# Feed-forward projections: one 512-column product for the weights' high part, and token factors moved to x's update

## The reference

```python
# first block (D_MODEL = 1024, D_FF = 4096)
h = rmsnorm(x, norm_mlp_g[i])
x = x + jnp.square(jax.nn.relu(h @ w_ff1[i])) @ w_ff2[i]
...
# second block, twice in each of its two layers (D_FF_2 = 2816, FFN_RES_WEIGHT = 0.5)
def swiglu(x, w_gate, w_up, w_down):
    return (jax.nn.silu(x @ w_gate) * (x @ w_up)) @ w_down

for layer in range(2):
    x = x + 0.5 * swiglu(rms_norm(x, norm_ffn1[layer]), ffn1_w_gate, ffn1_w_up, ffn1_w_down)
    xn = rms_norm(x, norm_mix[layer])
    x = x + mix(xn) @ w_out[layer]
    x = x + 0.5 * swiglu(rms_norm(x, norm_ffn2[layer]), ffn2_w_gate, ffn2_w_up, ffn2_w_down)
```

## Time and profile before

| what | value |
|---|---|
| median of 3 runs | 1515.05 us (1514.81 to 1521.53) |
| profiled execution, its own time | 1521.02 us |
| its span in the trace | 1519.2 us |
| TensorE busy | 1475.0 us (97%) |
| VectorE busy | 982.9 us (65%) |
| ScalarE busy | 721.0 us (47%) |
| mean granted TensorE clock | 0.991 |
| moved by DMA | 249.28 MB, mean 164 GB/s |

### The profile page before, as it was taken

The page is one execution under the profiler, slowest core; times in us unless marked ns, Lnnn a source line. Parts: engine busy times, 40 slices in busy tenths (PEclk is TensorE's granted clock), DMA queues, the critical chain, the costliest instruction groups (busy, mean ns, idle before and its releaser), DMA issues.

```text
span 1519.2 us, 25531 instructions
## 1 busy us (share of the span) xinstructions
PE 1475.0 (97%) x11068; PEld 1341.1 (88%) x11068; DVE 982.9 (65%) x1260; ACT 721.0 (47%) x864; POOL 0.2 (0%) x4
## 2 busy tenths in 40 slices
PE   7999999999998899998998999999999999899999
PEld 6999898998887899888778999899998777699987
DVE  5875577876457766557766665476654785576653
ACT  6743474543356543346555343363443564444432
POOL 0000000000000000000000000000000000000000
PEclk9999999999999999999999999999999998999999
DMA  7441135655544555544334555555555344155552
GB/s 301 158 163 58 57 112 194 211 173 195 193 164 141 193 193 172 190 166 167 134 116 159 176 193 179 189 184 174 191 182 190 127 164 142 30 192 185 176 194 83
DMA packets 35823, 249.28 MB, mean 164 GB/s; under 512 B 4096, under 2 KB 4224, under 8 KB 6144
## 3 DMA queue, kind: packets, MB, share of 16 engines
q1 hardware_dynamic: 35712, 247.65, 47.4%
HBM read 246.58 MB, written 1.05 MB: 163 GB/s over the span
## 4 chain that ended last, share of the span: by engine, by line
PE 93%; DVE 3%; ACT 2%; issue 1%; DMA 0%; SPq 0%; ACTq 0%; DVEq 0%
PE ps L1731 28%; PE ps L1733 28%; PE ps L1732 28%; PE ps L1861 2%; DVE lo L2413 1%; PE ps L1782 1%; ACT hi L2083 1%; PE ps L2028 1%; PE ps L2055 1%; PE ps L1890 1%; PE ps L2044 1%; PE ps L2036 1%; DMA X<-xin 0%; PE ps L1847 0%; PE ps L1985 0%
## 5 line engine op out<-in xcount | busy, mean ns | idle before, releaser
L2083 ACT CAST hi<-raw 128x2048 fp32r<-128x2048 f32 x230 | 437.8, 1905 | 556.7 <-PE ps L1733 553.5
L2413 DVE TENSOR_TENSOR lo<-raw,hi 128x2048 fp32r<-128x2048 f32 x230 | 526.4, 2290 | 268.0 <-ACT hi L2083 267.8
L1731 PE MATMUL ps<-HH,hi 128*128 128x256 f32 x2032 | 585.6, 288 | 19.6 <-DVE lo L2413 18.9
L1732 PE MATMUL ps<-HL,hi 128*128 128x256 f32 x2032 | 578.6, 285 | 0.0
L1733 PE MATMUL ps<-HH,lo 128*128 128x256 f32 x2032 | 578.5, 285 | 0.0
L1731 PEld LDWEIGHTS ps<-HH,hi 128*128 128x128 f32 x2032 | 393.5, 194 | 24.7 <-DVE lo L2413 20.7
L1732 PEld LDWEIGHTS ps<-HL,hi 128*128 128x128 f32 x2032 | 393.5, 194 | 0.2
L1733 PEld LDWEIGHTS ps<-HH,lo 128*128 128x128 f32 x2032 | 393.2, 193 | 0.0
L1731 PE MATMUL ps<-hi,a 128*128 128x512 f32 x584 | 231.1, 396 | 0.0
L1733 PE MATMUL ps<-hi,a 128*128 128x512 f32 x584 | 231.0, 396 | 0.0
L1732 PE MATMUL ps<-lo,a 128*128 128x512 f32 x584 | 229.9, 394 | 0.0
(11 more groups left out here) (310 smaller groups left out, 1200.1 us busy)
## 6 DMA issues: line engine op xcount, KB each, us to landing
raw<-ws SPq DMA_DIRECT2D x230, 1024.0 KB, 4.8
X<-xin SPq DMA_DIRECT2D x8, 256.0 KB, 6.4
const<-const SPq DMA_DIRECT2D x1, 1348.0 KB, 10.8
out<-X SPq DMA_DIRECT2D x4, 256.0 KB, 2.3
small<-small SPq DMA_DIRECT2D x1, 992.5 KB, 12.5
a<-row SPq DMA_DIRECT2D x1, 512.0 KB, 6.1
a<-pin SPq DMA_DIRECT2D x1, 256.0 KB, 5.3
const<-const SPq DMA_DIRECT2D x1, 64.0 KB, 2.6
```

Source lines behind the costliest of these rows:

```text
L1731: e.matmul(o, ah, bh, start=start, stop=False)
L1732: e.matmul(o, ah, bl, start=False, stop=False)
L2083: e.copy(hi[j % NSPL][:, :], raw[j % NRAW][:, :]).then_inc(hi_ready, 1)
L2413: e.tensor_tensor(lo[j % NSPL][:, :], raw[j % NRAW][:, :], hi[j % NSPL][:, :].bitcast(F), ALU.subtract).then_inc(lo_ready, 1)
```

## The change

- `HH` and `HL` become the two halves of one tensor `h2`. For gate, up and `w_ff1` a step (k, u) has two matmuls: the high part of the weights by both parts of h, 512 columns into a whole bank (first half high by high, second half high by low), and the low part of the weights by `HH`, 256 columns onto the first half. So each piece uses two banks.
- At the eviction the halves are added: ScalarE copies the second half of each bank to SBUF (new kind `half`), VectorE adds the first half to it (`add_halves`).
- The token factor is no longer applied to `up` and `relu`. `x_add` of the down projection multiplies with 0.5 * rstd or rstd squared instead, taken from columns that `n_root` and `f_end` now compute. `gate` still needs it ahead of the sigmoid and has a pass of its own for that. `relu` now squares in the same VectorE operation as the maximum, and ScalarE copies in place of squaring.
- `rows_into_x` clears `weaving[0]` before the next norm's parts follow.
- All other column pieces (23 of them) keep `cols_piece`.

```diff
-        HH = fixed("HH", [128, 8, S], R)
-        HL = fixed("HL", [128, 8, S], R)
+        h2 = fixed("h", [128, 2, 8, S], R)
+        HH, HL = h2[:, 0, :, :], h2[:, 1, :, :]
...
+        by_half = [st[:, 12:13], st[:, 13:14]]
+        by_square = [st[:, 14:15], st[:, 15:16]]
...
+        half_to = {"relu": rl, "gate": sgm, "up": ups}
...
-            emit("cols", pe=FINE * 0.36, i=i, a=j + 128 * u, o=0 if alone else u, k0=k, nk=nk, src=src, slot=slot,
-                 opens=k == 0 and (alone or u == 0), closes=k + FINE == nk and (alone or u == 1),
+            emit("wide" if wide else "cols", pe=FINE * 0.36, i=i, a=j + 128 * u, o=u, k0=k, nk=nk, src=src, slot=slot,
+                 opens=k == 0 and (wide or u == 0), closes=k + FINE == nk and (wide or u == 1),
...
+        def second_half(kind, slot, c, u, over):
+            return emit("half", act=0.4, slot=slot, to=kind, j=(c // 256) % 2, u=u, over=over, v=half_a.add())["v"]
+        def wide_piece(name, layer, c, needs, begin, evac):
+            piece_check(name, layer, 0, c)
+            i = next_piece[0]
+            yield from split(i)
+            sls = []
+            for u in range(2):
+                yield from room(1)
+                sls.append(take())
+                for k in range(0, 8, FINE):
+                    cols_step(i, 0, u, k, 8, "h", sls[u], needs, True)
+                    if k + FINE < 8:
+                        yield "pe"
+                begin(sls[u], c, u)
+                if u == 1:
+                    piece_done(i, sls[1])
+                    evac(sls[1], c, i + NSPL, sls[0])
+                    for sl in sls:
+                        give(sl)
+                yield "pe"
...
-                            if (half, u, k + FINE) == (1, 1, 8):
-                                piece_done(i0 + n, sls[n, 1])
+                            if k + FINE == 8:
+                                begin(sls[n, u], c, u)
+                                if u == 1:
+                                    piece_done(i0 + n, sls[n, 1])
...
                     give(sl[b, h])
                     if nm:
+                        weaving[0] = False
...
-                emit("x_add", dve=0.7, slot=sl, b=b, h=h, factor=factor, x=xt[b, h])
+                emit("x_add", dve=0.7, slot=sl, b=b, h=h, factor=factor[b], x=xt[b, h])
...
+        def relu_half(sl, c, u):
+            r_at[c, u] = second_half("relu", sl, c, u, f_at.get(c // 128 - 4))
+        def relu(sl, c, nxt, other):
             n = c // 128
-            emit("relu", slot=sl, other=other, n=n, v_r=ff_v.add(), v_hi=ff_a.add(), v=ff_v.add())
+            emit("relu", slot=sl, other=other, n=n, halves=(r_at[c, 0], r_at[c, 1]), v_r=ff_v.add(), v_hi=ff_a.add(), v=ff_v.add())
...
-        straight(rows_into_x("w_ff2", 0, 32, "s", lambda k, b: (ff_v.sem, f_at[k]), x_add(1.0), nm))
+        straight(rows_into_x("w_ff2", 0, 32, "s", lambda k, b: (ff_v.sem, f_at[k]), x_add(by_square), nm))
...
+            def gate_half(sl, c, u):
+                halves["gate", c, u] = second_half("gate", sl, c, u, at_.get(c // 128 - 4))
+            def up_half(sl, c, u):
+                halves["up", c, u] = second_half("up", sl, c, u, at_.get(c // 128 - 4))
+            def gate(sl, c, nxt, other):
+                sig[c] = emit("gate", slot=sl, other=other, halves=(halves["gate", c, 0], halves["gate", c, 1]), j=(c // 256) % 2, v_g=ff_v.add(), v=ff_a.add())["v"]
...
-            straight(rows_into_x(f"ffn{n}_w_down_2", layer, 22, "a", lambda k, b: (ff_v.sem, at_[k]), x_add(0.5),
+                    straight(wide_piece(wg, layer, c, nm.h_needs, gate_half, gate))
+                straight(wide_piece(wu, layer, c, nm.h_needs, up_half, up))
+            straight(rows_into_x(f"ffn{n}_w_down_2", layer, 22, "a", lambda k, b: (ff_v.sem, at_[k]), x_add(by_half),
                                  nxt_nm))
...
+                elif kind == "wide":
+                    j = s["i"] % NSPL
+                    wh = hi[j][:, :].rearrange("p (k n) -> p k n", k=8)
+                    wl = lo[j][:, :].rearrange("p (k n) -> p k n", k=8)
+                    if s["opens"]:
+                        e.wait_ge(lo_ready, s["i"] + 1)
+                        claim(sl)
+                    if s["need"]:
+                        e.wait_ge(s["need"][0], s["need"][1])
+                    a = s["a"]
+                    for k in range(s["k0"], s["k0"] + FINE):
+                        if k == 0:
+                            e.matmul(b2(sl), wh[:, k, a:a + 128], h2[:, :, k, :], start=True, stop=False)
+                            e.matmul(b2(sl)[:, 0, :], wl[:, k, a:a + 128], HH[:, k, :], start=False, stop=False)
+                        else:
+                            e.matmul(b2(sl)[:, 0, :], wl[:, k, a:a + 128], HH[:, k, :], start=False, stop=False)
+                            t = e.matmul(b2(sl), wh[:, k, a:a + 128], h2[:, :, k, :], start=False, stop=k == 7)
...
+                elif kind == "half":
+                    if s["over"]:
+                        e.wait_ge(ff_v.sem, s["over"])
+                    ready(sl)
+                    e.copy(half_to[s["to"]][s["j"]][:, s["u"], :], b2(sl)[:, 1, :]).then_inc(half_a.sem, 1)
                 elif kind == "relu":
                     n = s["n"]
-                    read_out(sl)
-                    e.activation(sH[:, n:n + 2, :], rl[(n // 2) % 2][:, :, :], ACT.Square).then_inc(ff_a.sem, 1)
+                    e.wait_ge(ff_v.sem, s["v_r"])
+                    e.copy(sH[:, n:n + 2, :], rl[(n // 2) % 2][:, :, :]).then_inc(ff_a.sem, 1)
...
-                    read_out(sl)
+                    e.wait_ge(ff_v.sem, s["v_g"])
...
+            def add_halves(s, to):
+                kind, j = s["kind"], s.get("j", s.get("n", 0) // 2 % 2)
+                for u, x in enumerate((s["other"], s["slot"])):
+                    e.wait_ge(half_a.sem, s["halves"][u])
+                    e.tensor_tensor(to[:, u, :], b2(x)[:, 0, :], half_to[kind][j][:, u, :], ALU.add).then_inc(free[x.b], 1)
+                read_out(s["other"])
+                read_out(s["slot"])
...
+                    e.wait_ge(rstd_ready.sem, s["v"])
+                    e.tensor_scalar(st[:, 12:14], st[:, 4:6], 0.5, None, ALU.mult)
+                    e.tensor_tensor(st[:, 14:16], st[:, 4:6], st[:, 4:6], ALU.mult)
...
-                    from_banks(sl, s["other"], lambda u, x: e.scalar_tensor_tensor(
-                        r[:, u, :], x, 0.0, RB2[:, u, :], ALU.max, ALU.mult))
+                    add_halves(s, r)
+                    e.scalar_tensor_tensor(r[:, :, :], r[:, :, :], 0.0, r[:, :, :], ALU.max, ALU.mult).then_inc(ff_v.sem, 1)
                     e.wait_ge(ff_a.sem, s["v_hi"])
-                    e.tensor_tensor(r[:, :, :], r[:, :, :], r[:, :, :], ALU.mult).then_inc(ff_v.sem, 1)
-                    e.wait_ge(ff_v.sem, s["v_r"])
...
-                    from_banks(sl, s["other"], lambda u, x: e.tensor_tensor(a[:, u, :], x, RB2[:, u, :], ALU.mult))
+                    add_halves(s, a)
+                    e.tensor_tensor(a[:, :, :], a[:, :, :], RB2, ALU.mult).then_inc(ff_v.sem, 1)
...
-                    from_banks(sl, s["other"], lambda u, x: e.tensor_tensor(g[:, u, :], x, RB2[:, u, :], ALU.mult))
-                    read_out(sl)
+                    add_halves(s, g)
```

More of the change, by code:

```diff
@@ L439, in program @@
         sgs = [ga_([128, 2, S]) for _ in range(2)]
+        ups = [ga_([128, 2, S]) for _ in range(2)]
+        half_to = {"relu": rl, "gate": sgm, "up": ups}
         ta = Arena(0)
@@ L569, in piece_check, with cols_step @@
             assert (n, ly, k0, c0) == (name, layer, kt, c), (plan[i], name, layer, kt, c)
-        def cols_step(i, j, u, k, nk, src, slot, needs, alone=False):
+        def cols_step(i, j, u, k, nk, src, slot, needs, wide=False):
             if src == "h":
@@ L603, in cols_piece, with wide_two @@
                 yield "pe"
-        def cols_two(jobs, needs, third=None):
+        def second_half(kind, slot, c, u, over):
[19 more added lines that the diff above has]
+                yield "pe"
+        def wide_two(jobs, needs, third=None):
             i0 = next_piece[0]
@@ L617, in cols_two @@
             for half in range(2):
-                for n, (name, layer, c, evac) in enumerate(jobs):
+                for n, (name, layer, c, begin, evac) in enumerate(jobs):
                     assert plan[i0 + n][:5] == (name, layer, 0, 8, c)
@@ L631, in cols_two @@
             if third:
-                name, layer, c, evac = third
+                name, layer, c, begin, evac = third
                 late = []
-                yield from cols_piece(name, layer, c, "h", needs, lambda sl, c, j: late.append((sl, c, j)))
+                yield from wide_piece(name, layer, c, needs, begin, lambda *args: late.append(args))
                 out(0)
@@ L1437, in program @@
         nm = Norm("norm_mlp_g")
-        straight(rows_into_x("w_out", 0, 8, "m", lambda k, b: (merge_v.sem, 2 * (k // 2) + 2), x_add(1.0), nm))
```

(29 more changed lines are left out.)

20 lines of the change are left out of this document (6 added, 14 removed).

## The result

The changed kernel takes 1496.92 us (median of 4 runs, 1494.63 to 1497.09) against 1514.93 us (4 runs) of the kernel before beside it: ratio 0.9863, 95% interval 0.9836 to 0.9889. That is 18.0 us faster. The forecast was 1489.6 us, range 1481 to 1502: the direction and the range held, the gain was 25.5 us by the forecast and 18.0 as measured. The profiled executions differ by 23.9 us (1521.02 and 1497.09 us); the forecast had 25.5 for this pair, 1495.5 us.

A forecast was written before the change was run, and what follows sets the result against it. TensorE, busy 97% of the span, was taken as the bound. Terms -18.4 - 7.5 - 3.9 + 2.3 + 0.5 + 1.2 + 0.3 = -25.5 us gave 1495.5 us profiled, 1489.6 us median, range 1481 to 1502.

The forecast's parts named there:

- The products: Column pieces on TensorE: a step costs 349 ns in place of 360, over 1664 steps -18.4 us.
- The rule with 2.5 ns: TensorE products: a removed matmul is worth only 2.5 ns, 4.2 us in all, total 1504; its rival had chance 0.13.
- rival of a slower two-part operand: Wide products: the 8 KB jump between halves of h costs time, each ns 1.66 us; chance 0.04.
- The evictions: VectorE and ScalarE emptying banks: added work stays covered at 81% and 59% busy in gate and up; zero.
- The flag: Two entries from attention into the second feed-forward: earlier splits remove waits, -7.5 us, and the clock gives back 3.9 us.
- The first gate and up: Entry after the final norm: six copies ahead of the sigmoid lengthen TensorE's wait, +2.3 us; saving of three pieces lost, +0.5.
- The clock at the first gate: After the longer wait in the first gate and up: half clock follows, +1.2 us, bounds 0 and 2.6.
- The factors: x_add reads its factor from a column, 0.747 in place of 0.690 us, 20 times: +0.3 us.
- The step from the profiled execution to the median: Whole kernel: the profiled execution was 6.0 us above the median of 1515.05, so 1495.5 became 1489.6 us.
- clock terms: Clock parts of the sum: -3.9 us at the entries after attention, +1.2 us at the first gate and up.

The follow-up runs named there:

- split run: Changed kernel with the 512-column product done as two of 256 for k = 1 to 6 of each group (1248 of 1664 steps): 1506.61 us.
- quarter products: Changed kernel with the 512-column product done as four of 128 columns for k = 1 to 6 of each group: 1753.98 us (one execution).
- contiguous run: Changed kernel with the two parts of h side by side per block k, 2 KB in one piece: 1499.11 us, ratio 0.9853.
- three later groups: Groups of follow-up runs, each with the kernel before measured beside them: medians of 1521.41, 1521.08 and 1520.85 us.
- run with the bank order: Changed kernel with the third piece's banks put at the end of the free list in the first gate and up: 1499.64 us, ratio 0.9851.

## Why the prediction was right, and by how much it was off

- **The products** (-18.4 us): right in mechanism and nearly in size. 104 pieces at 5.593 in place of 5.76 us are -17.4 us, 10.4 ns per step where the forecast had 11; the split run shows 8.3 ns for each step that it splits. What stands behind this price is not one fixed part of a product, as the quarter products show: 112, 120 and 229 ns for 128, 256 and 512 columns. It held only because both widths had been read from rows. The rule with 2.5 ns would have given 1504 us for the whole; it was wrong here. The rival of a slower two-part operand fell with the contiguous run.
- **The evictions** (zero): right within the stages. VectorE at 81%, ScalarE at 59%, additions 0.422 us and copies 0.372 us against 0.422 and 0.374 taken; one more pass in each of 44 evictions cost nothing either. Somewhere on the way into or through `w_ff1` something did cost: its 16 pieces bring 2.7 us, but the changed kernel gains only 1.9 (casts of the same hi at 222.19 and 362.88 before, at 222.49 and 361.28 after). No run shows what the 0.8 us are.
- **The flag** (-7.5 us of waits, -3.9 us of clock behind them): right. 8.5 us with the flag alone and 8.2 us when it is taken back, in span x clock; with the clock 12.0 us at the two entries by the positions of hi, against 11.4.
- **The first gate and up** (+2.3 and +0.5 us): right in size, in part by luck. TensorE started the fifth piece at 509.18 before and 510.31 after, with the entry 1.6 us sooner (first matmul on h at 477.50 and 475.90): 2.7 us lost. The cause was half right: ScalarE's queue, yes, but its block grew by 1.65 us (7.15 against 5.5), not by 2.2; and the last thing waited for was a bank, which is 1.0 us of the wait. `wide_piece` gives the third piece's banks back in the script ahead of those of the first two, though they are emptied last, and with two banks per piece the fifth piece meets them. The forecast counted banks ("two in place of one per piece, of eight") and not their order. It also put the idle time before at 1.9 us and after at about 3.7; the rows have 1.66 and 4.00.
- **The clock at the first gate** (+1.2 us): the term of the sum that was sized wrong. Behind the wait of 4.00 us the clock took 2.45 us. With the 2.7 us that is 5.2 us at this entry, where the forecast had 4.0. That the losses by the yardstick are nearly the same before and after (14.0 and 13.7) doesn't mean that the entries after attention gave nothing back: what went there came in at the first gate, and the yardstick counts the slow stretch at 491.69 to 494.26 too, which delayed nothing.
- **The factors** (+0.3 us): x_add takes 750 ns against 747 taken; the term is too small to be seen.
- **The step from the profiled execution to the median** (-6.0 us): this is the step that failed, and nearly the whole of the 7.3 us between 1489.6 and 1496.92. I took 6.0 us off because the profiled execution stood so far above the median of its three runs, and assumed the changed kernel would do likewise. It stood at its median (1497.09 and 1496.92). In the three later groups the kernel before had medians of 1521.41, 1521.08 and 1520.85, near the profiled execution. Of these 27 executions four took 1513.8 to 1515.6 us, with a granted clock of 0.993 or 0.994; the others had 0.987 to 0.991. So the 6 us were most likely the clock of the two low executions behind the median of 1515.05 (theirs is not on record), and no property of a profiled one.

The pair of profiled executions comes out with 23.9 us against 25.5: short by 1.0 for the products, 1.2 at the first gate and 0.8 around `w_ff1`; over by 0.6 at the entries after attention, and by 1.6 that are luck, the slow stretch in attention which only the profiled execution before has of these two. Those make 24.7; the 0.8 us left are open. Without the luck this pair has 22.3 us against 25.5. The means of span x clock, which leave the clock out, have 23.1 (1504.6 - 1481.5), where the forecast without its clock terms has 22.8; that this agrees so closely is partly chance, as errors above cancel.

Open: which slow stretches an execution gets. They differ between executions of one kernel (13.7 and 19.1 us lost), and the length of the idle time alone doesn't settle it: the wait of 2.18 us at the first gate was followed by one in the changed kernel (490.73) and by none in the run with the bank order (490.23).

## What to carry to other kernels

Before pricing a merged or a split matmul, find the price by columns from starts in the trace, at more than one width: here 112, 120 and 229 ns for 128, 256 and 512 columns, so that halving a 512 costs 8 to 11 ns and quartering it over 200. When an edit adds work in front of an eviction, look at the one place where evictions are already queued (an entry that works ahead), and at the order in which banks come back; there the change cost more than its own duration, and reordering that entry gave 6 to 8 us by the ratios (0.9821 and 0.9808 against 0.9862, of 1521 us). Compare span x granted clock beside the medians: two effects of 8 us here were plain in it and blurred by 5 us in the medians. For effects of 1 to 3 us take its mean over all executions, or the start of the same instruction in two traces; and before you trust the distance between a profiled execution and the median, look at the clock of each.

## What the runs showed of the hardware

- Four matmuls of 128 columns and one of 256, each with weights of its own, take 0.56 us together: 112 ns each. From 256 columns (120 ns) down to 128 there is next to nothing to save.
- Two halves 8 KB apart in SBUF feed a 512-column matmul as fast as 2 KB in one piece: 14 pieces take 78.30 and 78.31 us.
- At the lower clock a step of one 512- and one 256-column product takes 0.64 us. Its 768 columns, one per clock, are 640 ns at 1.2 GHz by estimate, and 320 at 2.4, where the step takes 347: the part over the stream shows at full clock only.
- After idle times of 2.18 and 4.00 us TensorE's clock was at its lower level while matmuls ran again (16 of them in 5.23 in place of 2.78 us); in another run a wait of 2.18 us at the same place was not followed by it. The time lost to it differs between executions of the same kernel by over 5 us, as much as several of the effects under study.
